# Turning k and q and scoring the first heads between the groups of the last projection chunk

## What is computed

```python
proj = x @ w_in                       # qa ka va qb kb vb gate_pre
qa = apply_axial_rope(rms_heads(qa, q_gain), cos, sin)
ka = apply_axial_rope(rms_heads(ka, k_gain), cos, sin)
ya = gqa_axial_attention(qa, ka, va) @ w_branch_a      # full softmax(q k^T) v
yb = dilated_window_attention(qb, kb, vb, ...) @ w_branch_b   # three dilations
gates = sigmoid(gate_pre + b_gate)
merged = g_a * ya + g_b * yb
x = layer_norm(ALPHA * x + merged @ w_out, ln1_g, ln1_b)
x = layer_norm(ALPHA * x + hierarchical_moe(x, ...), ln2_g, ln2_b)
```

## Time and profile before

| | us |
|---|---|
| median of 3 runs | 1344.36 (1343.69 to 1345.16) |
| the profiled execution, its own time | 1342.55 |
| its span, first to last instruction | 1340.9 |
| PE busy | 1258.2 (94%) |
| DVE busy | 701.3 (52%) |
| ACT busy | 622.6 (46%) |
| mean granted clock of TensorE | 0.975 of full speed |

### The profile page before, as it was taken

How to read it: one execution, slowest core, us unless ns; L and a number is a source line. 1 busy time by engine, 2 the same in 40 slices (tenths; PEclk the granted TensorE clock), 3 DMA queues, 4 the chain that set the end, 5 groups by cost and what they waited for, 6 DMA issues and landing times.

```text
span 1340.9 us, 19105 instructions
## 1 busy us (share of the span) xinstructions
PE 1258.2 (94%) x7182; PEld 1033.8 (77%) x7183; DVE 701.3 (52%) x890; ACT 622.6 (46%) x844; POOL 345.2 (26%) x306
## 2 busy tenths in 40 slices
PE   5999899999999999989999999679999999989992
PEld 4888867788878888956788878667788888878871
DVE  4233367422476333267512474868755765785456
ACT  4222376533233222277632240767754665775445
POOL 0532000000120232000000030147643746575333
PEclk9999999999999999999999999589999999999997
DMA  6742200033463322200012544479977978898553
GB/s 219 254 148 95 95 1 2 1 95 107 145 220 126 126 95 94 95 32 1 1 63 79 173 141 178 137 248 296 348 263 212 308 234 294 265 352 281 178 184 151
DMA packets 63521, 212.33 MB, mean 158 GB/s; under 512 B 12390, under 2 KB 12902, under 8 KB 62647
## 3 DMA queue, kind: packets, MB, share of 16 engines
q1 hardware_dynamic: 49052, 178.24, 38.5%
q0 software_dynamic: 11808, 24.59, 7.1%
q10 hardware_dynamic: 2592, 8.53, 1.6%
HBM read 199.00 MB, written 34.25 MB: 174 GB/s over the span
## 4 chain that ended last, share of the span: by engine, by line
PE 83%; DVE 5%; ACT 3%; POOL 3%; issue 3%; DMA 2%; SPq 0%; POOLq 0%; ACTq 0%; DVEq 0%
PE banks L737 22%; PE banks L739 22%; PE banks L738 22%; PE banks L903 2%; PE banks L867 2%; PE banks L938 2%; PE banks L1021 2%; PE banks L945 2%; PE banks L878 1%; PE banks L771 1%; POOL gated L607 1%; DMA moe_raw<-in_expert_w 1%; POOL moe_lo L665 1%; PE banks L1044 1%; ACT qkvA L1247 1%
## 5 line engine op out<-in xcount | busy, mean ns | idle before, releaser
L1465 DVE TENSOR_TENSOR wlo<-raw,whi 128x2048 fp32r<-128x2048 f32 (+1 forms) x52 | 116.0, 2231 | 183.9 <-ACT whi L1137 183.9
L1446 DVE TENSOR_TENSOR moe_lo<-moe_raw,moe_hi 128x2048 fp32r<-128x2048 f32 x81 | 183.4, 2287 | 32.5 <-ACT moe_hi L1294 30.3
L1294 ACT ACTIVATE moe_hi<-moe_raw 128x2048 fp32r<-128x2048 f32 x96 | 182.8, 1916 | 32.2 <-PE banks L739 19.6
L737 PE MATMUL banks<-xT,whi 128*128 128x512 f32 x448 | 175.7, 392 | 0.0
L738 PE MATMUL banks<-xT,whi 128*128 128x512 f32 x448 | 175.3, 391 | 0.0
L739 PE MATMUL banks<-xT,wlo 128*128 128x512 f32 x448 | 175.1, 391 | 0.0
L607 POOL TENSOR_TENSOR gated<-gated,kqv 128x512 f32<-128x512 f32 x16 | 25.3, 1597 | 496.6 <-DVE kqv L1607 496.6
L737 PE MATMUL banks<-moe_lo,xeh 128*128 128x512 f32 x368 | 146.5, 398 | 4.1 <-DVE moe_lo L1446 2.5
L737 PE MATMUL banks<-wlo,xT 128*128 128x256 f32 (+1 forms) x448 | 135.2, 302 | 13.3 <-DVE wlo L1465 13.3
L738 PE MATMUL banks<-moe_hi,xeh 128*128 128x512 f32 x368 | 144.8, 393 | 0.0
L739 PE MATMUL banks<-moe_hi,xel 128*128 128x512 f32 x368 | 144.8, 393 | 0.0
(11 more groups left out here) (273 smaller groups left out, 2321.2 us busy)
## 6 DMA issues: line engine op xcount, KB each, us to landing
moe_raw<-in_expert_w SPq DMA_DIRECT2D x192, 512.0 KB
raw<-in_front_w SPq DMA_DIRECT2D x104, 512.0 KB, 4.9
toeplitz_rows<-bias_rows POOLq DMA_DIRECT2D x4, 1152.0 KB, 13.7
kqv<-in_x_turned SPq DMA_DIRECT2D x8, 512.0 KB, 7.8
pt<-in_x SPq DMA_DIRECT2D x2, 2048.0 KB, 10.3
x_rows<-pt ACTq DMA_DIRECT2D x8, 512.0 KB, 2.7
token_sums<-pt ACTq DMA_DIRECT2D x8, 512.0 KB, 3.8
moe_raw<-token_sums SPq DMA_DIRECT2D x8, 512.0 KB, 8.7
```

The lines of the kernel that those rows point to most:

```text
L737: mm(dst, left[0], right[1], start=first, stop=False)
L1294: A(moe_hi[m % SPLIT_E], moe_raw[m % RAW_E], ACT.Copy).then_inc(e_hi, 1)
L1446: V.tensor_tensor(moe_lo[m % SPLIT_E], moe_raw[m % RAW_E], moe_hi[m % SPLIT_E].bitcast(F32), ALU.subtract).then_inc(lo_sem(m % ECH), 1)
L1465: V.tensor_tensor(view(lo, shape), view(raw[c % 2], shape), view(hi, shape).bitcast(F32), ALU.subtract).then_inc(w_split, 1)
```

## The change

1. On PE, chunk 11 is taken out of the chunk loop and its four groups are interleaved with other work: both tiles of k are turned, group 0, q tiles 0 and 1, group 1, a wait for three tiles of `qkA_ready` and for `logit_ready`, `scores(0)`, q tiles 2 and 3, groups 2 and 3. Only then come the waits for all of q, k and the values, and the loop, now without `scores(0)`.
2. The order of `TR_ORDER` and `turned_by` becomes k before q.
3. On ACT the work on chunk 11 becomes: copy out k 0 and k 1, group 0, q 0 to 3, the two exponentials of p = 0, group 2. On DVE the maximum of p = 0 comes between the copies of groups 1 and 3.
4. The split of chunk 13 leaves its place at the end of chunk 11. On ACT and on DVE it now stands behind the attention, right before the loop over the gate chunks.

```diff
-    TR_ORDER += [("q", _s, _t) for _t in range(TT)] + [("k", _s, u) for u in range(2)]
+    TR_ORDER += [("k", _s, u) for u in range(2)] + [("q", _s, _t) for _t in range(TT)]
...
-    return "qkA_ready", (TT + 2) * key[1] + (TT if key[0] == "k" else 0) + key[2] + 1
+    return "qkA_ready", (TT + 2) * key[1] + (2 if key[0] == "q" else 0) + key[2] + 1
...
-                for c in range(1, N_QKV):
+                for c in range(1, N_QKV - 1):
                     for g in range(qkv_groups(QKV[c])):
...
+                def last_chunk(t):
+                    by_token(N_QKV - 1, MM_QKV[N_QKV - 1] + t, t, xT_v)
+
+                pe.wait_ge(tab_act, N_TAB // 2)
+                pe.wait_ge(tab_dve, N_TAB // 2)
+                pe.wait_ge(q_turned, s * 3 + 3)
+                pe.wait_ge(ident_in, 16)
+                turn_k(0)
+                turn_k(1)
+                last_chunk(0)
+                turn_q(0)
+                turn_q(1)
+                last_chunk(1)
+                pe.wait_ge(qkA_ready, s * 6 + 3)
+                pe.wait_ge(logit_ready, s * TT + 2)
+                scores(0)
+                turn_q(2)
+                turn_q(3)
+                last_chunk(2)
+                last_chunk(3)
+                pe.wait_ge(qkA_ready, s * 6 + 6)
+                pe.wait_ge(va_ready, s * TT + TT)
+                pe.wait_ge(b_act, s * 12 + 12)
+                pe.wait_ge(b_dve, s * 12 + 12)
                 for p in range(NP + 2):
-                    if p < NP:
+                    if 0 < p < NP:
                         scores(p)
...
+                    elif c < N_QKV - 1:
+                        keep_v(q, 0)
+                        keep_v(q, 2)
                     else:
...
+                        act.wait_ge(tab_out, 16)
+                        keep_k(0)
+                        keep_k(1)
+                        keep_v(q, 0)
+                        for u in range(TT):
+                            keep_q(u)
+                        exps(0)
+                        keep_v(q, 2)
...
-                    if c + 2 < N_CHUNK:
+                    if c < N_QKV - 1:
                         split_hi(c + 2)
...
                 act.wait_ge(const_in, CONSTS)
+                split_hi(C_GATE + 1)
                 for c in range(C_GATE, N_CHUNK):
...
+                            if (c, t) == (N_QKV - 1, 1):
+                                logits_of(0)
...
-                    if c + 2 < N_CHUNK:
+                    if c < N_QKV - 1:
                         split_lo(c + 2)
...
                 for p in range(NP + 4):
-                    if p < NP:
+                    if 0 < p < NP:
                         logits_of(p)
...
+                split_lo(C_GATE + 1)
                 for c in range(C_GATE, N_CHUNK):
```

More of the change, by code:

```diff
@@ L836, in _ @@
                                 else by_token(c, MM_QKV[c] + g, g, xT_v))
[L839 to L858, removed]
                 halves = [slice(v * HD, (v + 1) * HD) for v in range(2)]
@@ L955, in turn_den, with turn_k, turn_q @@
                     last.then_inc(den_turned, 1)
+                def turn_k(u):
+                    b = tr_open(("k", s, u))
+                    for v in range(2):
+                        last = nc.tensor.transpose(b[:, v * P:(v + 1) * P], k_rot[:, 2 * u + v, :], ident)
+                    last.then_inc(tr_done, 1)
+                def turn_q(t):
+                    b = tr_open(("q", s, t))
+                    for m in range(4):
+                        last = nc.tensor.transpose(b[:, m * P:(m + 1) * P],
+                                                   q_rot[:, t, m].rearrange("p v d -> p (v d)"), ident)
+                    last.then_inc(tr_done, 1)
+                def last_chunk(t):
[21 more added lines that the diff above has]
+                pe.wait_ge(b_dve, s * 12 + 12)
                 for p in range(NP + 2):
-                    if p < NP:
+                    if 0 < p < NP:
                         scores(p)
@@ L1161, in _, with keep_k, keep_q, keep_v @@
                     keep_x1(s - 1, 3)
+                def keep_k(u):
+                    b = tr_wait(("k", s, u))
+                    A(kA[:, u * 256:(u + 1) * 256], b[:, 0:256], ACT.Copy).then_inc(qkA_ready, 1)
+                def keep_q(u):
+                    b = tr_wait(("q", s, u))
+                    A(qA[:, :, u * P:(u + 1) * P], b.rearrange("p (m n) -> p m n", m=4), ACT.Copy).then_inc(qkA_ready, 1)
+                def keep_v(q, t):
+                    b = mm_wait(MM_QKV[QKV.index(q)] + t)
+                    A(vB[:, t, q - 9, :, 0:HD], b[:, 0:256].rearrange("p (h d) -> p h d", h=B_HEADS), ACT.Copy).then_inc(b_act, 1)
+                def exps(p):
+                    act.wait_ge(a_max, s * N_MAX + maxes_by(p) + 1)
+                    for v in range(2):
+                        k = 2 * (p % 2) + v
+                        A(probs[p % 2][v][0], bank[score_bank(p, v)][:, :], ACT.Exp, bias=neg_max[:, k:k + 1], scale=1.0,
+                          accum_out=den_of(p, v)).then_inc(a_exp, 1)
                 for c in range(N_QKV):
@@ L1187, in _ @@
                         A(dst, b[:, :], ACT.Copy, scale=-SCALE if f < 6 else 1.0).then_inc(b_act, 1)
-                    else:
[L1189 to L1192, removed]
+                    elif c < N_QKV - 1:
+                        keep_v(q, 0)
+                        keep_v(q, 2)
+                    else:
+                        act.wait_ge(tab_out, 16)
[6 more added lines that the diff above has]
+                        keep_v(q, 2)
                     if q in (3, 4, 5):
@@ L1236, in _ @@
                     if p < NPA:
[L1237 to L1241, removed]
+                        if p > 0:
+                            exps(p)
                     elif p < NP:
@@ L1472, in logit, with logits_of @@
                                     b_route, ALU.add).then_inc(logit_ready, 1)
+                def logits_of(p):
+                    k = 2 * (p % 2)
+                    if p < NPA:
+                        dve.wait_ge(sc_done, s * N_SCORE + scores_by(p) + 1)
+                        V.tensor_reduce(neg_max[:, k:k + 2], two[3 - p % 2].rearrange("p (v n) -> p v n", v=2), X, ALU.max,
+                                        negate=True).then_inc(a_max, 1)
+                        return
+                    t, hp = (p - NPA) // 2, p % 2
+                    done = s * N_LOGIT + 2 * (p - NPA)
+                    dve.wait_ge(sc_done, s * N_SCORE + scores_by(p) + 1)
+                    for v in range(2):
+                        h = 2 * hp + v
+                        w = probs[p % 2][v][1]
+                        V.tensor_tensor_reduce(w[:, 0:512], bank[6 + v][:, :], tabs[:, h, 3 - t:7 - t].rearrange("p b n -> p (b n)"),
+                                               1.0, 3.0e38, ALU.add, ALU.min, half_min[:, k + v:k + v + 1]).then_inc(b_logit, 1)
+                    dve.wait_ge(b_logit, done + 2)
+                    dve.wait_ge(sc_done, s * N_SCORE + scores_by(p) + 2)
+                    for v in range(2):
+                        h = 2 * hp + v
+                        w = probs[p % 2][v][1]
+                        V.tensor_tensor_reduce(w[:, 512:768], bank[4 + v][:, 0:256], tabs[:, h, 7:9].rearrange("p b n -> p (b n)"),
+                                               1.0, half_min[:, k + v:k + v + 1], ALU.add, ALU.min,
+                                               neg_max[:, k + v:k + v + 1]).then_inc(a_max, 1)
                 if s == 0:
```

## The result

The changed kernel took 1335.45 us (median of 4 runs, 1333.54 to 1336.59), the kernel before 1344.51 us beside it (4 runs). The ratio on record is 0.9944, with an interval from 0.9929 to 0.9960: faster, by 5.4 to 9.5 us, which is under 1% and clear of the noise. The two medians taken alone lie 9.06 us apart, a ratio of 0.9933; that is inside the interval. The forecast was 1337.3 us, within 1335.0 to 1341.0. The profiled execution took 1336.53 us for a span of 1334.9, 6.0 us less than before.

A forecast was written before the change was run, and what follows sets the result against it. PE's work is 83% of the last-ending chain, so its idle time counts. The hand-over takes 9.48 instead of 13.03 us, 3.55 us less a sequence, 7.1 in all: 1344.36 - 7.1 = 1337.3 us, range 1335.0 to 1341.0.

The forecast's parts named there:

- The bound and the place: PE's work is 83% of the last-ending chain; time won on PE in the hand-overs should reach the end.
- The sum: PE from the end of chunk 11's own work to `scores(3)`: 9.48 instead of 13.03 us, 3.55 us less a sequence.
- 20 transposes and `scores(0)` among the groups: Inside chunk 11 on PE: turns of q and k cost 2.2 us, the early score 1.06 us.
- from group 3 to `scores(1)`: In front of the attention loop, PE newly waits 0.67 us for DVE's copy of group 3.
- `scores(1)` to `scores(3)`: First loop passes on PE take 5.55 us, with a 0.12 us wait before `turn(1)`, which takes 1.26 us.
- What was costed at nothing: Earlier `q_turned`, copies of k and q, exponentials of p = 0 and chunk 13's moved split cost PE no time.
- covers: Time by which helper work in chunk 11 precedes PE's need: 0.4 us for k's copies, 1 us or more elsewhere.
- Rival 3: ACT's copies slip in chunk 11 or first passes wait longer; half the gain is lost: 1340.8 us, chance 0.13.
- Rival 2: Chunk 13's split comes 5.1 us late, behind chunk 12's sigmoids: 1347.5 us; chance 0.04 together with the slower-clock rival.
- Rival 1: Small work among groups lowers PE's clock, 3.4 us a fall: 1344.1 to 1350.9 us; 0.04 with the late-split rival.
- The rule on transposes: Trainium skill rule: PE-mode transposes do not count as PE work for the clock gate; it would favour a clock fall.
- the largest gain of the sum: Upper bound if the new wait before the loop nearly vanishes: 4.2 us a sequence, 8.4 us in all.

The follow-up runs named there:

- the late split: Changed kernel with ACT's split of chunk 13 behind both sigmoids of gate chunk 12 instead of ahead: median 1350.76 us, ratio 1.0051 to the kernel before.
- the second profile: The kernel before, unchanged, profiled once more: end of chunk 10 to gate chunk 12 took 110.73 and 111.69 us; span 1340.2 us.

## Why the prediction was right

**The bound and the place.** Right. What was won on PE in the hand-overs reached the end: from gate chunk 12 to the next hand-over the changed kernel took 300.08 us, the kernel before 300.01 (557.29 - 257.28). In the two profiled executions the ways differ by 3.36 + 3.38 = 6.74 us and the spans by 6.0 us; the rest is chiefly the stretch up to the end of chunk 10, which took 146.99 us instead of 146.54. That stretch lay between 146.67 and 147.29 us in three profiles of the changed kernel.

**The sum.** Its 3.55 us a sequence measured 3.37 us. By its steps, in the first sequence:

| step | forecast | measured |
|---|---|---|
| 20 transposes and `scores(0)` among the groups | 2.2 + 1.06 = 3.26 | 161.87 - 146.99 - 11.52 = 3.36 |
| from group 3 to `scores(1)` | 0.67 | 162.64 - 161.87 = 0.77 |
| `scores(1)` to `scores(3)` | 5.55 | 168.18 - 162.64 = 5.54 |
| all | 9.48 | 9.67 |

The turns did cost 0.11 us each: eight of them took 0.79 us to the next group's start (150.30 to 151.09), as in the earlier trace rows; the eight behind `scores(0)` took 0.84 us (155.20 to 156.04). The 0.10 us more lies chiefly at `scores(0)`, which began 0.21 us behind the last matmul of group 1 where 0.12 was to be expected (153.93 to 154.14). The wait was 0.10 us longer at its end: DVE's copy began 0.20 us behind the end of the group (162.07) and took 0.42 us, both as worked out, but PE went on 0.15 us behind the copy, not 0.05. The passes of the loop came to the hundredth, with the wait of 0.12 us and the long `turn(1)`.

**What was costed at nothing.** `q_turned`, the copies and the exponentials all kept their covers, the thinnest being that of k: 0.65 us instead of 0.4, because two copies took 0.64 us and not 0.84. The split of chunk 13 had 4.5 us of slack where 4.4 were worked out; the late split shows that the slack is all that hides it.

**Rivals.** Rival 3 did not come. Rival 2 was excluded by the code and holds as a mechanism. Rival 1, that the change brings the clock down, did not show in any of the fourteen hand-overs profiled with the turns interleaved and the split behind the attention (seven profiles, each kernel's ways alike to 0.02 us). The rule on transposes that the prediction sets beside it did not show either: the 20 transposes stood among the groups at a granted clock of 1.00. That the trace of before "agrees" with the rule was no support, since that trace shows no fall. The rival's argument against, "the old hand-over ran at 1.00 in spite of its gaps", was weak too: one profile was taken for the rule. In the second profile the clock did fall in the old hand-over. A fall seen here cost 0.96 to 2.8 us, not the 3.4 us that the rival took from the earlier trace rows. The fall was seen with the old hand-over's gaps and not without them; that it can't come in the new one isn't shown.

**The total.** The forecast's 7.1 us stand between 6.7 us by the two ways and the 7.4 to 8.1 us of the three ratios (0.9945 to 0.9940). The median of 1335.45 us lies 1.85 us under the forecast. It is below the 1336.0 us that the largest gain of the sum, 8.4 us, would give, and inside the range only by the 1 us that was allowed for the spread of the medians; that part of the hit is luck, and the sum is judged by the ways. Falls of the clock in the old hand-over, one in four seen, 0.96 us, go in that direction: they would add some 0.5 us on average. That they make up the whole difference isn't shown; 0.9950 lies in all three intervals.

**What the gain is made of.** By the ways, the split's move alone gives 1.30 us a sequence; turns among the groups together with that move give 2.39 us; the early score adds 0.98 us. The parts depend on each other: the interleaving without the move gives 0.96 us in an undisturbed sequence (110.74 - 109.78).

## What to carry to other kernels

When PE passes from one stage to the next, put the small work that starts the new stage between the last groups of the old one, as long as the banks and tiles allow it. Then look at each helper engine's queue for long work that was hidden in the old order: here it was a split in DVE's queue, with its wait for ACT's half, that took 2.41 of 3.37 us back. For changes of some tenths of a per cent, measure from one fixed instruction to another in the profile; here that repeated to 0.02 us where the clock stayed up, while the runs of one kernel spread over 4 us and more. Take a second profile before a place is called safe from the clock.

## What the runs showed of the hardware that was not expected

**The same idle time does not always cost the same.** The hand-over before held 3.6 us of idle time in 13 us, in gaps of at most 1.61 us. In three of four cases the granted clock stayed at 2.4 GHz, in the fourth it went to 1.2 GHz and cost 0.96 us. Behind a wait of 2.45 us it fell in one of two sequences (3.99 us lost instead of 2.41). Behind a pause of 5 us it fell both times, and cost 2.8 and 1.7 us beyond the pause. The two hand-overs with only the split moved held 2.3 us of idle time (0.31, 0.20, 0.47 and 1.28 us) and stayed at 1.00.

The Trainium skill (TensorE: Matmul & The Clock Gate, Part 1) has the gate's window run on its own, not from the kernel's start, which would make such falls differ from run to run. The traces agree in so far as two profiles of one program differ in the same place; they don't show the cause.

**The load of a table took 1.28 us and no more.** In the changed kernel ACT's copies ended at 156.98, the load began at 156.99 and the exponential at 158.29. The Trainium skill (ScalarE: Activation LUTs, What ACT_TABLE_LOAD costs) counts a drain of about 1.38 us besides; the trace does not show it here, and the measurement decides.
